# Convolution inside the choice of keys, rotation inside the state space, row unit first in the projections, and dummy identity turns at four places

## What is computed

```python
# first block
q, k, v, iq, ik, iw, z, xbc, dt_raw = split(x @ w_in)
q, k, iq, ik = rope(q), rope(k), rope(iq), rope(ik)
sc = sum_h(relu(iq_h @ ik.T) * iw_h), causal; keep the 256 best keys of each query
att = softmax attention over the kept keys
xbc = silu(causal_conv4(xbc) + conv_b)         # depthwise, four taps
y   = ssd(xbc, softplus(dt_raw + dt_bias), a_log) + d_skip * xs
ssd = rms(y * silu(z)) * norm_w
x = layer_norm(ALPHA * x + concat(att, ssd) @ w_out); x = layer_norm(ALPHA * x + moe(x))
# second block, per layer
proj = rms_norm(h) @ w_in; o = concat(neighbourhood, latent, window attention of proj)
h = h + rms_norms(o) @ w_out; h = h + expert_choice_ffn(rms_norm(h))
```

## Time and profile before

| what | value |
|---|---|
| three runs | 3968.12, 3970.08, 3979.78 us; median 3970.08 |
| the profiled execution, its own time | 3970.15 us |
| its span, first to last instruction | 3968.3 us |
| mean granted PE clock | 0.928 |
| PE / DVE / ACT / POOL busy | 87% / 66% / 52% / 10% of the span |
| `project_index` | 0 to 74 us |
| tables and rotation of the index chunks | 75 to 93 us |
| `choose_keys` | 94 to 338 us |
| tables, rotation of the others, convolution | 339 to 396 us |
| `state_space`, first stage / second stage | 396 to 414 / 414 to 492 us |
| `attend_pairs` of the first block | 492 to 634 us |
| `project_two`, first layer | 1205 us on |

### The profile page before, as it was taken

How to read it: one execution, slowest core, us unless ns; L and a number is a source line. 1 busy time by engine, 2 the same in 40 slices (tenths; PEclk the granted TensorE clock), 3 DMA queues, 4 the chain that set the end, 5 groups by cost and what they waited for, 6 DMA issues and landing times. The chain is left out here.

```text
span 3968.3 us, 53782 instructions
## 1 busy us (share of the span) xinstructions
PE 3447.9 (87%) x18166; PEld 2552.0 (64%) x18166; DVE 2631.8 (66%) x4360; ACT 2054.9 (52%) x3310; POOL 389.7 (10%) x302
## 2 busy tenths in 40 slices
PE   7995798779946998999599999789989995999996
PEld 3442466667735865567478888669555674888884
DVE  1696664578864246565589999641655645999996
ACT  0571363168843245444277777531554442777774
POOL 0001300012231000100011111110000000111110
PEclk9997889889978999999799999989999996999998
DMA  2100002277543110002399999631100024999997
GB/s 89 65 1 11 7 1 97 83 293 264 202 158 128 49 29 23 27 1 81 134 344 382 393 384 382 255 120 33 29 22 27 1 105 163 362 382 382 382 389 275
DMA packets 122204, 650.36 MB, mean 164 GB/s; under 512 B 14112, under 2 KB 22688, under 8 KB 70048
## 3 DMA queue, kind: packets, MB, share of 16 engines
q1 hardware_dynamic: 101568, 573.48, 37.2%
q0 software_dynamic: 15984, 58.20, 5.1%
q10 hardware_dynamic: 4464, 16.25, 1.0%
HBM read 585.50 MB, written 62.39 MB: 163 GB/s over the span
## 5 line engine op out<-in xcount | busy, mean ns | idle before, releaser
L3226 DVE TENSOR_TENSOR low_ring<-mix,high_ring 128x2048 fp32r<-128x2048 f32 x256 | 576.9, 2285 | 41.3 <-ACT high_ring L3175 41.3
L3175 ACT ACTIVATE high_ring<-mix 128x2048 fp32r<-128x2048 f32 x256 | 477.8, 1937 | 80.3 <-PEq L125 80.3
L3116 PE MATMUL ps<-high_ring,x_high 128*128 128x512 f32 x1024 | 410.1, 400 | 14.7 <-DVE low_ring L3226 7.4
L3118 PE MATMUL ps<-high_ring,x_low 128*128 128x512 f32 x1024 | 401.1, 392 | 0.0
L3117 PE MATMUL ps<-low_ring,x_high 128*128 128x512 f32 x1024 | 400.6, 391 | 0.0
L3226 DVE TENSOR_TENSOR low_ring<-more_raw,high_ring 128x2048 fp32r<-128x2048 f32 x128 | 290.3, 2287 | 27.9 <-ACT high_ring L3175 27.9
L3175 ACT ACTIVATE high_ring<-more_raw 128x2048 fp32r<-128x2048 f32 x128 | 247.0, 1930 | 0.0
L3116 PEld LDWEIGHTS ps<-high_ring,x_high 128*128 128x128 f32 x1024 | 193.2, 189 | 78.3 <-DVE low_ring L3226 20.2
L3118 PEld LDWEIGHTS ps<-high_ring,x_low 128*128 128x128 f32 x1024 | 193.1, 189 | 41.5
L3117 PEld LDWEIGHTS ps<-low_ring,x_high 128*128 128x128 f32 x1024 | 193.3, 189 | 38.0
L3116 PE MATMUL ps<-high_ring,h_high 128*128 128x512 f32 x512 | 205.2, 401 | 0.0
(11 more groups left out here) (487 smaller groups left out, 8035.4 us busy)
## 6 DMA issues: line engine op xcount, KB each, us to landing
mix<-in_expert_units SPq DMA_DIRECT2D x256, 1024.0 KB, 7.9
more_raw<-in_expert_units SPq DMA_DIRECT2D x128, 1024.0 KB, 8.8
raw_experts<-in_expert_units SPq DMA_DIRECT2D x16, 3072.0 KB, 11.5
expert_out<-out ACTq DMA_DIRECT2D x31, 512.0 KB, 2.7
mix<-in_w_turned SPq DMA_DIRECT2D x20, 512.0 KB, 3.7
feats<-residual SPq DMA_DIRECT2D x16, 512.0 KB, 7.1
qk_tail<-in_w_out SPq DMA_DIRECT2D x8, 1024.0 KB, 8.3
mix<-residual SPq DMA_DIRECT2D x16, 512.0 KB, 3.3
```

The lines of the kernel that those rows point to most:

```text
L3116: nc.tensor.matmul(ps[:, bank, :], left_high, high, start=first, stop=False)
L3118: return nc.tensor.matmul(ps[:, bank, :], left_low, high, start=False, stop=final)
L3175: nc.scalar.activation(w_high[:, n % RING, :], raw[n % RAW_UNITS], ACT.Copy).then_inc(high_ready, 1)
L3226: nc.vector.tensor_tensor(w_low[:, n % RING, :], raw[n % RAW_UNITS], w_high[:, n % RING, :].bitcast(F32), ALU.subtract).then_inc(low_ready, 1)
```

## The change

What it does, part by part.

**Tables.** `rotate_chunks` and both of its `load` stages go. The turner, cosine and sine are loaded once, on the queue of `project_index` behind its own loads; cosine and sine lie in the not yet used half of `heads_out`. `rotate` is called for the index chunks only.

**Choice of keys.** All scores come first, then all 30 groups; the six xbc chunks are now first. ACT copies a group after two of every three bits. DVE convolves one xbc chunk before bits 26, 23, 20, 18, 16 and 14 of its bisection, in place; `low_key` is made after bit 17 where it was bit 12. ACT takes the silu of the sums behind its own bisections, and the silu of z as it copies z out. `convolve` goes. The constants of the state space are loaded on this stage's queue.

```diff
+    chunk_order = list(range(FIRST, M)) + list(range(FIRST))
+    groups = [(m, h) for m in chunk_order for h in range(2)] + [(None, t) for t in range(T)]
+    convolve_before = {26: 0, 23: 1, 20: 2, 18: 3, 16: 4, 14: 5}
...
-            for what, i in order:
-                if what == "project":
...
+            for i in tiles:
                 keys = (i + 1) * P
...
+            for i in range(len(groups)):
+                project(i)
...
-                nc.scalar.activation(out, ps[:, 4 + i % 4, :], ACT.Copy).then_inc(kept, 1)
+                nc.scalar.activation(out, ps[:, 4 + i % 4, :], ACT.Silu if m is None else ACT.Copy).then_inc(kept, 1)
...
-                    if b % 2 == 0 and later:
+                    if b % 3:
                         keep(later.pop(0))
...
+            act.wait_ge(taps_in, 16 * (2 + len(meanwhile)))
+            for m in range(XBC_CHUNKS):
+                if later:
+                    keep(later.pop(0))
+                act.wait_ge(summed, m + 1)
+                nc.scalar.activation(xbc[:, m, 0:S], xbc[:, m, 0:S], ACT.Silu, bias=tap_bias[:, m:m + 1])
...
+            def convolve(m):
+                taken = halves(xbc[:, m, 0:S])
+                dve.wait_ge(kept, 2 * m + 2)
+                chain.step(nc.vector.tensor_scalar(acc, halves(xbc[:, m, 1:1 + S]), taps[:, m, 1:2], None, ALU.mult))
+                for j in range(2, CONV):
+                    chain.step(nc.vector.scalar_tensor_tensor(out=acc, in0=halves(xbc[:, m, j:j + S]),
+                                                              scalar=taps[:, m, j:j + 1], in1=acc, op0=ALU.mult,
+                                                              op1=ALU.add))
...
             for b in range(30, -1, -1):
+                if b in convolve_before:
+                    convolve(convolve_before[b])
...
-                if b == 12:
+                if b == 17:
```

```diff
+                turn_chunk(0)
                 for g in range(T * 2):
...
                 pe.wait_ge(read, T * 2)
+                turn_chunk(1)
+                turn_chunk(2)
                 pe.wait_ge(adt_ready, 1)
...
+                turn_chunk(3)
+                turn_chunk(4)
...
+                pool.wait_ge(adt_ready, 1)
+                for n in range(2, len(order)):
+                    nc.gpsimd.tensor_tensor(halves(by_cos[:, n, :]), halves(raw[:, order[n], :]), cos,
+                                            ALU.mult).then_inc(cos_done, 1)
...
+                by_cosine(0)
...
+                by_sine(0)
...
+                add(0)
+                by_sine(1)
...
+                by_cosine(1)
+                add(1)
+                for n in (2, 3, 4):
+                    by_sine(n)
+                    add(n)
```

```diff
-    units = [("chunk", m) for m in rotated_chunks]
-    units += [("rows", 0), ("chunk", 0), ("rows", 1), ("chunk", 1), ("rows", 2), ("chunk", 2), ("chunk", 3)]
+    units = [("rows", 0)] + [("chunk", m) for m in rotated_chunks]
+    units += [("chunk", 0), ("rows", 1), ("chunk", 1), ("rows", 2), ("chunk", 2), ("chunk", 3)]
...
-            for t in range(5):
-                split_tile(t)
+            keep_busy(nc, ps[:, 3, 0:P], ident, 56)
+            split_tile(0)
+            split_tile(1)
...
-                pe.wait_ge(split_low, T if g < 2 else 2 * T)
+                pe.wait_ge(split_low, 2 * min(g + 1, T))
...
+                if g + 2 < T:
+                    split_tile(g + 2)
```

```diff
+def keep_busy(nc, out, ident, turns):
+
+    for _ in range(turns):
+        nc.tensor.transpose(out, ident[:, :], ident[:, :])
...
+                keep_busy(nc, ps[:, 6, 0:P], ident, 28)
                 turn_x(0)
+                keep_busy(nc, ps[:, 6, 0:P], ident, 20)
```

More of the change, by code:

```diff
@@ L265, in _ @@
                 for h in range(2):
-                    last = nc.tensor.matmul(ps[0:parts, 2 * (n % 4) + h, :], turner[0:parts, 0:parts],
-                                            raw[0:parts, order[n], tile(h, HALF)], start=True, stop=True)
+                    last = nc.tensor.matmul(ps[:, 2 * (n % 4) + h, :], turner[:, :], raw[:, order[n], tile(h, HALF)],
+                                            start=True, stop=True)
                 last.then_inc(full, 1)
@@ L876, in search @@
                     chain.step(ins)
-                    if b % 2 == 0 and later:
+                    if b % 3:
                         keep(later.pop(0))
             n = 0
-            for what, i in scoring:
-                if what == "project":
-                    keep(i)
-                    continue
+            for i in tiles:
                 keys = (i + 1) * P
@@ L1106, in _, with turn_chunk @@
             @block.tensor
             def _(pe):
+                def turn_chunk(n):
+                    if n >= 3:
+                        pe.wait_ge(sin_done, n - 2)
+                    for h in range(2):
+                        last = nc.tensor.matmul(ps[:, TURNED[n] + h, :], turner[:, :], raw[:, order[n], tile(h, HALF)],
+                                                start=True, stop=True)
+                    last.then_inc(turned_full, 1)
+                turn_chunk(0)
                 for g in range(T * 2):
@@ L2636, in split_of, with keep @@
                                          ACT.Copy).then_inc(split_high, 1)
+            def keep(g):
+                u, part = groups[g]
+                kind, m = units[u]
+                act.wait_ge(full, g + 1)
+                if kind == "rows":
+                    nc.scalar.activation(rows_out[:, part, tile(m, W)], ps[:, bank_of[g], 0:W], ACT.Copy)\
+                        .then_inc(read, 1)
+                else:
+                    nc.scalar.activation(qk[m][:, tile(part, HALF)], ps[:, bank_of[g], :], ACT.Copy).then_inc(read, 1)
             split(0)
@@ L2647, in _ @@
                     split(1)
+                if t >= 3:
+                    keep(t - 3)
             split_of(T - 1)
-            for g, (u, part) in enumerate(groups):
-                kind, m = units[u]
+            for g in range(T - 3, len(groups)):
+                u, part = groups[g]
                 if part == 0 and 1 <= u and u + 1 < len(units):
                     split(u + 1)
-                act.wait_ge(full, g + 1)
-                if kind == "rows":
-                    nc.scalar.activation(rows_out[:, part, tile(m, W)], ps[:, g % BANKS, 0:W], ACT.Copy)\
-                        .then_inc(read, 1)
-                else:
-                    nc.scalar.activation(qk[m][:, tile(part, HALF)], ps[:, g % BANKS, :], ACT.Copy).then_inc(read, 1)
+                keep(g)
         @block.gpsimd
```

267 lines of the change are left out of this document (123 added, 144 removed).

## The result

The changed kernel ran at 3905.73, 3909.1, 3908.9 and 3907.52 us, median 3908.21; the kernel before at a median of 3969.45 us in four runs. The ratio is 0.9841, 95% interval 0.983 to 0.9853. The forecast was 3905 us, from 3880 to 3928. The profiled execution took 3905.73 us, with a span of 3903.6 us, 64.7 us less than before.

The account below looks back on a forecast made before the run. The prediction took TensorE (PE), busy for 87% of the span, as the bound. Its terms, -7.0 + 7.0 - 50.5 - 1.5 - 8.0 - 4.4 = -64.4 us from 3970.15, gave 3905.8, rounded to 3905 us; range 3880 to 3928.

Parts of the forecast that it names:

- The large term: PE's last group through state space's first stage: rotation and convolution stages go, -57.5 us, first stage +7; net -50.5.
- The convolution's cover: In choose_keys: convolution on DVE costs nothing, ending about 326 us, before PE's end at 337; margin 11 us.
- Scores: In choose_keys: scores without groups between stay at the low clock, +7.0 us; the groups cost 206 us either way.
- rival 1: In choose_keys: scores run at the high clock, sum 12.9 us less, 3893 us; chance 0.25.
- project_two: Two layers: first product 6.8 us sooner, partly lost to added turns and a colder start; -4 per layer, -8.0.
- Turns: Dummy turns sometimes raise PE's clock: -1.5 us before attention; latent_heads -1.2 and experts -1.0 for each layer.
- Rival 2: Before attention, in latent_heads and experts: turns raise no clock, 13.3 us more, 3919 us; chance 0.12.
- Rival 3: In choose_keys: the clock stays low in the groups, 13.7 us each, all 30 some 4110 us; chance 0.02.
- Rival 4: In choose_keys: convolution not hidden, DVE ends after PE, about 3922 us; counted with the forecast, no separate chance.

Follow-up runs that it names:

- group_weights: Changed kernel with one projection group behind the scores of tile 3 and project_two's third weight load ahead of the last two row tiles and tables; median 3891.6 us.
- group_weights_no_turns: `group_weights` with all dummy turns left out; median 3900.74 us over four runs.
- best: Changed kernel with one group behind tile 3, project_two's third weight load early, and the second turner product ahead of the state space's turns; median 3889.28 us.
- one_group: Changed kernel with one projection group behind the scores of tile 3, the other 29 behind tile 7; 3901.64 us, one run.
- two_groups_weights: Changed kernel with projection groups behind the scores of tiles 3 and 5 and project_two's third weight load early; 3891.18 us over four runs.
- conv_twice: Changed kernel with DVE doing the first three of the four convolution steps of each chunk twice; 3916.99 us.

## Why the prediction was right, and where its terms were off

The sum of -64.4 us met -64.7 in the profile; the medians differ by 61.2. The large term was right by its own steps: rotation and convolution stages away, the state space's first stage 7 us longer (7.5 measured), -50.5 forecast and -50.6 found. The convolution's cover was forecast at 11 us from DVE's last mask to PE's last group and is 9.9 (10.8 to the next stage); doubling most of the convolution and putting groups back between the scores both used it up and cost 10 to 12 us.

Other terms were off and cancelled. That the sum came out within a microsecond is luck:

- **Scores.** I took the low clock throughout, +7.0, and got +1.7 between the first score and PE's last group. That is two things in one number. From the first score to the first group behind tile 7, without the groups between, the scores went from 29.5 to 38.8 us: +9.3, where my own 30.9 and 42.6 say +11.7. The direction was right (0.50 until tile 7), and tile 7 at 1.00 took off the rest. But the groups went from 213.8 to 206.3 us: -7.6, which I had at nothing ("206 us either way"). I had written that PE waits only between heads; in fact it stood 3.03 us for ACT's copy, with the clock down behind it, 4.7 us in all, and the group behind tile 3 had run at the low clock for its first part (8.7 us instead of 6.9). My sum did not add up either: 206 + 42.6 is 248.6, 5.2 us and not 7.0 above the 243.4 measured, and 206 + 30.9 falls 6.5 us short of it, and looking for those 6.5 us would have led me to the wait.
- **The clock in the scores.** It rises at a moment that differs by execution: at tile 5, at the first pair of tile 7 or at the second. All profiles without a group lie between the forecast (low throughout) and rival 1 (high throughout), within 6.3 us of each other, and neither of the two occurred as written.
- **The range.** Its lower end should be 3893 - 4 - 6 = 3883, not 3880; nothing hangs on it.
- **project_two.** I took -4 us a layer and layer 1 gave -2.4. The first product came 7.1 us sooner, as worked out (6.8). What I had not followed is ACT's queue: the load of the third weights stands behind two row tiles and eight tables on SP, ACT's split of it ahead of the square of row tile 6, and PE behind that, 2.99 us in layer 1 and 12.0 - 8.1 = 3.9 in layer 2. The step asked what delays the first product and not who is queued behind the next load.
- **Turns.** Summed at -1.5 - 2.4 - 2.0 = -5.9, they measured -5.1 and -9.2 in two pairs of profiles and -9.1 between medians, all of it with scatter of some microseconds. The place was partly wrong: the sixty before the attention give nothing (140.13 and 140.23 us, and 141.75 and 141.71). They raise the clock (1.00 from 430 us to their end at 434.64), but behind 2.86 us of idle time the attention's first products run at 0.50, from 437.5 to 455.3 us.
- **Rival 2**, that transposes raise no clock, is refuted. In the 56 turns behind 70.08 us of idle time the granted clock was 0.50 for the first 4 us and 0.99 after:

```profile
1149.50:1153.50 4.00, 3.98 (x19) 4.00 (x20) 0.00 (x0) 1.10 (x1) 0.00 (x0) 0.50 0.20 48
1153.50:1157.80 4.30, 4.28 (x39) 4.04 (x37) 1.23 (x1) 1.07 (x1) 0.00 (x0) 0.99 0.99 358
```

  These are 19 turns, then 39. The sentence of the Trainium skill, "TensorE: Matmul & The Clock Gate", "Part 4: PE-mode transpose", doesn't hold for these float32 transposes. The time agrees: behind the first attention the two kernels without turns took 5.1 and 9.2 us longer, not less.
- **Rival 3**, a low clock through the groups, did not occur: with 81 records in 35.03 us and 74 in 31.92 they ran as before.
- **Rival 4**, an uncovered convolution, is refuted by the 10.78 us of DVE's wait.

## What to carry to other kernels

Work moved onto an engine beside a bound one is free up to that engine's slack at the end of the stage, so count what feeds it first: here the convolution was hidden because the scores that DVE waits for came ahead of PE's filler work. When the first product of a stage is brought forward, read the queue of every engine for the next load and what stands behind the wait for it; moving one load ahead of two row tiles and the tables gave 9.5 us over two layers, where the reordering had given 2.4 in the first. When a stage is longer than its parts add up to, look for a wait in the middle of it: here one of 3.03 us on the bound engine had gone unread. And compare stages across traces before comparing totals: at 0.1% a single run tells more about when the clock rose than about the edit.

## What I had not expected of the hardware

- With identical code in front of it, the granted clock rose during the scores at 107, at 119, or at about 124 us, worth up to 6.3 us of the stage; and behind a full-array group at 1.00 it fell to between 0.50 and 0.53 in three profiles (`group_weights`, `group_weights_no_turns`, `best`) and held in two (`one_group`, `two_groups_weights`).
- Short stops of PE were followed by the low clock: 3.03 us in the groups of the kernel before (0.50 from 247.3 to 249.5 us), 3.02 us in `conv_twice` (0.50 from 233.8 to 237 us), 2.99 us in `project_two` (0.50 from 1188.8 to 1190.4 us) and 2.86 us before the attention (0.50 for the next 18 us).
- POOL's product of two SBUF tensors blocks a DVE operation of 64 columns for its whole length (0.2 us became 2.2 to 2.4), also one with a single tensor input.
- Turns of one identity tile ran at 0.21 us each in the first 19 of `project_two` (4.0 us) and at 0.11 us behind them.
